# A decoder trunk step on one core: who sums the squares at the three phase boundaries, and with what the third unit opens

## The chip, the cores and the metric

One Trainium2 chip, one of its cores. The metric is the device time of one execution in microseconds (us), the median of the runs shown. Engines: TensorE (PE, with its weight loads as PEld), VectorE (DVE), ScalarE (ACT), GpSimd (POOL) and SyncE (SP), which issues most DMAs.

## The reference

One inference step of a two-layer trunk over 544 tokens (512 prompt tokens and 8 samples of 4), model width 1024, feed-forward width 2816. Cut to what matters:

```python
def rms_norm(x, g):
    y = x * rsqrt(mean(x * x, axis=-1) + EPS) * g

for l in range(2):
    h = rms_norm(x, norm_mix_pre[l])
    mix = mixer_ab(h, ...) if l == 0 else mixer_c(h, ...)     # in_ab/out_ab, in_c/out_c
    x = x + rms_norm(mix, norm_mix_post[l])
    h = rms_norm(x, norm_ffn_pre[l])
    a, b = split(h @ w_up)
    fo = (gelu(conv3(a)) * b) @ w_down                         # up0/down0, up1/down1
    x = x + rms_norm(fo, norm_ffn_post[l])
```

So in front of each of up0, in_c and up1 there are two norms in a row: the post-norm of the phase that ends, whose result is added to x, and the pre-norm of the new x, which feeds the next projection.

## The kernel before, in words

Activations lie feature by token: 8 row tiles (k = 0 to 7) of 128 partitions by 544 tokens. A bank of PSUM holds 272 columns of float32 here, so the tokens are cut in two halves, t = 0 and t = 1 (`cols(t)`). Every product is made of three passes of a split number, h_hi x w_hi, h_lo x w_hi and h_hi x w_lo, in `half` (L435 to L454). A *unit* is 128 output features over all k; its two halves e = 0, 1 are four k each, 24 products of 272 columns. Units use the accumulators `acc[0]` and `acc[1]` in turn (u % 2), each of two banks, one for each t. The semaphore `evac` counts accumulators that VectorE has emptied; before unit u PE waits until unit u-2 has been emptied (L681).

Eight phases follow each other: in_ab, out_ab, up0, down0, in_c, out_c, up1, down1. PE, VectorE, ScalarE and GpSimd each run their own program in order; what comes first on an engine is the order written out in its block, and all else is semaphores.

**The pre-norm is applied behind the projection.** h_hi and h_lo hold x times the gain, without the root; the results are multiplied by `rstd` when they leave PSUM. So products of the next phase start before the norm is known. The norm needs, for each half t, the sum of squares over all 1024 features: ScalarE writes the squares to `sq_c` (L1082, signal `sq_pre`); PE sums them in `square_sums` (L520 to L529), eight products with a 128 x 32 matrix of ones into four groups of 32 partitions, so that four partial sums stand there 32 times each; ScalarE copies this to `S[2]` (`sums_out`, L920, signal `sums_taken`); PE sums over partitions with a 128 x 128 matrix of ones (`pre_stats`, L531 to L534, signal `stat_done`); ScalarE makes the root with Ln and Exp (`norm_root`, L911 to L918, signal `rstd_ready`). Since every sum is then held 32 times, the scale in Ln is 1/(32 D).

**The first two units** of such a phase are interleaved with these steps (`first_pair`, L478 to L512): first all of t = 0 for both units, as its h tiles come, with the last post-norm statistics `stats(norm - 1, 1)` behind four of its products; then `square_sums` of t = 0; then t = 1, k by k for both units, with `pre_stats` of t = 0 behind k = 4, `square_sums` of t = 1 ahead of k = 7, and `pre_stats` of t = 1 at the end. VectorE copies each accumulator out whole (L1413), unscaled, and multiplies by `rstd` when the root is there (L1678 in up phases, L1836 in in_c). `third_unit` (L514) waits for the first of these copies, then makes the first half of the third unit.

**What follows in an up phase.** Units 2j and 2j+1 make the two sides of gate pair j. For each pair, in this order: VectorE empties the even unit times rstd into `S[0]` (L1700; for pair 0 it is the copy and L1678), GpSimd takes the columns of the samples (L1994 to L1998), ScalarE makes one tap of the convolution (L1170), VectorE the others (L1382 to L1386), ScalarE the gelu (L1174), GpSimd multiplies it with rstd (L2042), VectorE empties the odd unit times this (L1706; for pair 0 L1682), ScalarE rounds it to g_hi (L1180), VectorE subtracts (L1708, L1684). Between these stand the splits of the weights to come: ScalarE rounds (L876), VectorE subtracts (L1364), half a unit at a time. Unit 4 waits for L1700 of unit 2, unit 5 for L1706 of unit 3.

**In in_c** a head is four units; behind the units of the first head PE makes transposes (L808) of `kd`, at the end of a chain of scans and exponentials on VectorE and ScalarE that starts at L1836.

ScalarE's and VectorE's sides of the boundaries are `after_out` (behind out_ab and out_c) and `after_down` (behind down0).

Of the kernel before, what the change touches and what calls it, by code (L numbers as in the profile page):

```python
# [173 lines left out]
def build(nc, dram):  # L174
# [11 lines left out]
    with ctx:  # L186
# [119 lines left out]
        sq_summed, sums_taken = sem("sq_summed"), sem("sums_taken")  # L306
        stat_done = sem("stat_done")
# [126 lines left out]
        def _(pe):  # L434
# [43 lines left out]
            def first_pair(name, norm):  # L478

                m = 2 * UNIT0[name]  # L480
                if norm == 0:
                    for k, u in [(0, 0), (1, 0), (0, 1), (1, 1)] + [(k, u) for k in range(2, 8) for u in range(2)]:
                        e = k // 4
                        half(m + 2 * u + e, 0, u, h, 4 * e, e == 0, e == 1, tile_ready(0) if u == 0 else None,
                             ks=[k % 4], signal={(0, 3): 1, (0, 7): 1, (1, 7): 2}.get((u, k), 0))
                    for t in range(2):
                        stats(0, t)
                    return
                pre = norm // 2
                if pre == 2:  # L490
                    pe.wait_ge(evac, TILE0[name] - 1)
                for e in range(2):
                    for u in range(2):
                        if (e, u) == (0, 1):
                            pe.wait_ge(mix_cols, COLS0[pre + 1])
                        for k in range(4):
                            half(m + 2 * u + e, 0, u, h, 4 * e, e == 0, e == 1, half_ready(pre, 0) if u == 0 else None,
                                 ks=[k], signal=0, ts=(0,))
                        if (e, u) == (0, 0):
                            stats(norm - 1, 1)  # L500
                square_sums(pre, 0)
                pe.wait_ge(evac, TILE0[name])
                for k in range(8):
                    e = k // 4
                    if k == 7:
                        square_sums(pre, 1)
                    for u in range(2):
                        half(m + 2 * u + e, 0, u, h, 4 * e, e == 0, e == 1, half_ready(pre, 1) if u == 0 else None,
                             ks=[k % 4], signal={(0, 3): 1, (0, 7): 1, (1, 7): 2}.get((u, k), 0), ts=(1,))
                    if k == 4:  # L510
                        pre_stats(pre, 0)
                pre_stats(pre, 1)  # L512

            def third_unit(name):  # L514

                m = 2 * (UNIT0[name] + 2)
                pe.wait_ge(evac, TILE0[name] + 1)
                half(m, 0, 0, h, 0, True, False)

            def square_sums(pre, t):  # L520

                sq = sq_c
                pe.wait_ge(rstd_ready, 4 * pre - 2 + t + 1)
                for k in range(KD):
# [4 lines left out]
                mm.then_inc(sq_summed, 1)  # L529
# [145 lines left out]
            def ffn(layer):  # L675
# [10 lines left out]
                third_unit(name)  # L686
                half(2 * (UNIT0[name] + 2) + 1, 0, 0, h, 4, False, True)
# [169 lines left out]
        def _(act):  # L857
# [53 lines left out]
            def norm_root(norm, out, t):  # L911

                pre = norm % 2 == 0 and norm > 0
                src = A[2 + t if pre else t][:, 0:H]
                act.wait_ge(stat_done, 2 * norm + t + 1)
                step.mark(act.activation(out[:, cols(t)], src, ACT.Ln, bias=eps[:], scale=1.0 / (32 * D if pre else D)))
# [3 lines left out]
            def sums_out(pre, t):  # L920

                act.wait_ge(sq_summed, 2 * pre - 1 + t)
                act.copy(S[2][:, cols(t)], A[2 + t][:, 0:H]).then_inc(sums_taken, 1)

# [159 lines left out]
            def after_out(out, post, gain, name):  # L1084
# [19 lines left out]
                for k in range(KD):  # L1104
                    normed_tile(pre, 1, k, gain)
                    normed_square(1, k)
                    if k == 4:
                        sums_out(pre, 0)
                norm_root(2 * pre, rstd, 0)
                sums_out(pre, 1)  # L1110
                norm_root(2 * pre, rstd, 1)

            def after_down(post, gain=None, name=None):
# [20 lines left out]
                norm_root(post, S[3], 1)  # L1134
                for k in range(KD):
                    normed_tile(pre, 1, k, gain)
                    normed_square(1, k)
                    if k == 4:
# [213 lines left out]
        def _(dve):  # L1352
# [65 lines left out]


# [248 lines left out]
            def ffn(layer):  # L1668
                name = f"up{layer}"

                def first_unit(t):

                    pair = CA + KF * layer
                    if t == 1:
                        dve.wait_ge(sp_ready, pair)
                        first_pair(name, (S[0][:], S[3][:]))
                        dve.wait_ge(rstd_ready, 2 * (3 + 4 * layer))
                        dve.tensor_tensor(S[0][:], S[0][:], rstd[:], ALU.mult).then_inc(rescaled, 1)  # L1678
# [32 lines left out]
                base = step.n  # L1711
                up(0, 0, True)
                per = step.n - base
                base = step.n
# [114 lines left out]
            def head_out(t, cur):  # L1829
# [3 lines left out]
                if isinstance(cur, int) and cur == 0 and t == 1:  # L1833
                    first_pair("in_c", (S[0][:], qn[:]))
                    dve.wait_ge(rstd_ready, 10)
                    dve.tensor_tensor(S[0][:], S[0][:], rstd[:], ALU.mult).then_inc(rescaled, 1)  # L1836
# [338 lines left out]
```

## Time and profile before

| | us |
|---|---|
| median of 3 runs | 1331.42 (1331.3 to 1331.63) |
| profiled execution, own time | 1331.55 |
| its span in the profile | 1329.8 |
| PE busy | 1309.1 (98%) |
| DVE busy | 802.4 (60%) |
| ACT busy | 595.7 (45%) |
| POOL busy | 187.0 (14%) |

TensorE's granted clock is at its upper level, 2.4 GHz, throughout (0.998 in the mean). Products are pipelined: a row of 0.29 us stands for one product of 272 columns, but the next begins 0.125 us later, so for PE the distance between starts counts and not the duration. A row "x2" groups two products. A bracket "[0.66 <-ACT ...]" at the end of a row is the engine's idle time before it and what ended it.

### The profile page before, as it was taken

What the parts mean: (1) busy time and instruction counts of PE and PEld (TensorE: products, weight loads), DVE (VectorE), ACT (ScalarE), POOL (GpSimd) and SP (SyncE); (2) the same over time, 40 slices, a digit from 0 to 9 for tenths busy, and PEclk for the clock granted to TensorE, in tenths of its full rate; (3) what the DMA queues carried; (4) which work ended last, traced back from release to release, by engine and by line L of the source; (5) the groups of instructions that cost most, each with busy time, mean ns of one, the idle gap of its engine ahead of it and who ended that gap; (6) DMA issues with size and microseconds to landing.
All of it is one profiled execution on the core that took longest, in us unless ns stands there. A gap on an engine that the chain in (4) does not pass through costs nothing.

```text
span 1329.8 us, 31828 instructions
## 1 busy us (share of the span) xinstructions
PE 1309.1 (98%) x12588; PEld 1278.5 (96%) x12588; DVE 802.4 (60%) x1458; ACT 595.7 (45%) x1207; POOL 187.0 (14%) x320
## 2 busy tenths in 40 slices
PE   9999999999999999999999999999999999999997
PEld 9988999999999999997999999989999999999996
DVE  6476576655655632238988888968565565552224
ACT  5367355333333322237666666646433333332231
POOL 0111121111111100000211111111111111120000
PEclk9999999999999999999999999999999999999999
DMA  8311221323222322212333233331123322332212
GB/s 293 116 49 65 82 95 51 92 95 92 81 82 92 123 89 88 81 50 87 115 110 99 97 97 103 108 118 60 53 90 95 93 80 81 98 122 89 89 41 68
DMA packets 39685, 123.23 MB, mean 93 GB/s; under 512 B 4232, under 2 KB 12168, under 8 KB 39496
## 3 DMA queue, kind: packets, MB, share of 16 engines
q1 hardware_dynamic: 35400, 111.92, 26.7%
q10 hardware_dynamic: 4048, 10.00, 2.2%
q8 instruction: 44, 0.72, 0.2%
q0 software_dynamic: 176, 0.44, 0.1%
q14 instruction: 17, 0.14, 0.0%
HBM read 113.78 MB, written 8.57 MB: 92 GB/s over the span
## 4 chain that ended last, share of the span: by engine, by line
PE 91%; DVE 4%; ACT 2%; issue 1%; DMA 0%; POOL 0%; ACTq 0%; SPq 0%; DVEq 0%
PE acc L449 85%; PE aux L753 1%; DVE w_lo L1364 1%; PE aux L606 1%; PE aux L781 0%; PE aux L737 0%; DVE x L1586 0%; DMA raw<-in_w_in_ab 0%; DVE mix L1581 0%; PE aux L527 0%; PE aux L628 0%; PE aux L618 0%; DVE h_lo L1373 0%; ACT w_hi L876 0%; PE aux L545 0%
## 5 line engine op out<-in xcount | busy, mean ns | idle before, releaser
L1364 DVE TENSOR_TENSOR w_lo<-raw,w_hi 128x512 fp32r<-128x512 f32 (+1 forms) x372 | 305.4, 825 | 321.9 <-ACT w_hi L876 321.8
L449 PE MATMUL acc<-h_hi,w_hi 128*128 128x272 f32 x2208 | 474.5, 293 | 3.3 <-DVE h_lo L1373 2.5
L449 PE MATMUL acc<-h_hi,w_lo 128*128 128x272 f32 x2208 | 464.7, 288 | 0.0
L449 PE MATMUL acc<-h_lo,w_hi 128*128 128x272 f32 x2208 | 463.3, 288 | 0.5 <-issue 0.5
L449 PEld LDWEIGHTS acc<-h_hi,w_hi 128*128 128x128 f32 x2208 | 349.6, 188 | 15.4 <-issue 7.5
L876 ACT CAST w_hi<-raw 128x512 fp32r<-128x512 f32 (+1 forms) x372 | 236.3, 642 | 264.1 <-PE acc L449 258.4
L449 PEld LDWEIGHTS acc<-h_lo,w_hi 128*128 128x128 f32 x2208 | 349.9, 189 | 0.2
L449 PEld LDWEIGHTS acc<-h_hi,w_lo 128*128 128x128 f32 x2208 | 348.0, 189 | 0.6 <-issue 0.6
L449 PE MATMUL acc<-g_hi,w_hi 128*128 128x272 f32 x704 | 153.0, 288 | 0.0
L449 PE MATMUL acc<-g_hi,w_lo 128*128 128x272 f32 x704 | 153.0, 289 | 0.0
L449 PE MATMUL acc<-g_lo,w_hi 128*128 128x272 f32 x704 | 152.4, 288 | 0.0
L449 PEld LDWEIGHTS acc<-g_hi,w_hi 128*128 128x128 f32 x704 | 113.4, 188 | 0.1
L449 PEld LDWEIGHTS acc<-g_lo,w_hi 128*128 128x128 f32 x704 | 113.4, 189 | 0.1
L449 PEld LDWEIGHTS acc<-g_hi,w_lo 128*128 128x128 f32 x704 | 112.7, 189 | 0.0
L2042 POOL TENSOR_TENSOR scratch<-scratch,rstd 128x544 f32<-128x544 f32 x44 | 60.0, 1364 | 169.1 <-ACT scratch L1174 169.1
L1174 ACT ACTIVATE scratch<-scratch 128x544 f32<-128x544 f32 x44 | 29.0, 659 | 112.3 <-DVE scratch L1386 112.3
L1180 ACT CAST g_hi<-scratch 128x544 f32 (+1 forms) x44 | 28.5, 647 | 98.2 <-DVE scratch L1706 93.7
L449 PE MATMUL acc<-y_hi,w_hi 128*128 128x272 f32 x256 | 69.9, 292 | 1.7 <-DVE y_lo L1889 1.3
L449 PE MATMUL acc<-y_hi,w_lo 128*128 128x272 f32 x256 | 68.9, 288 | 0.0
L449 PE MATMUL acc<-y_lo,w_hi 128*128 128x272 f32 x256 | 68.8, 288 | 0.0
L1170 ACT ACTIVATE scratch<-scratch,vec 128x544 f32<-128x544 f32 x44 | 33.0, 751 | 65.7 <-DVE scratch L1700 64.0
L1987 POOL TENSOR_TENSOR scratch<-scratch 128x272 f32<-128x272 f32 (+1 forms) x30 | 31.2, 1038 | 198.6 <-ACT scratch L1036 151.2
(255 smaller groups left out, 1339.6 us busy)
## 6 DMA issues: line engine op xcount, KB each, us to landing
raw<-in_w_up SPq DMA_DIRECT2D x88, 512.0 KB, 3.6
raw<-in_w_down SPq DMA_DIRECT2D x32, 704.0 KB, 4.1
raw<-in_w_in_c SPq DMA_DIRECT2D x32, 512.0 KB, 3.7
raw<-in_w_in_ab SPq DMA_DIRECT2D x18, 512.0 KB, 3.8
raw<-in_w_out_ab SPq DMA_DIRECT2D x8, 512.0 KB, 3.6
S<-in_state ACTq DMA_DIRECT2D x8, 512.0 KB, 3.6
o_ss<-Snew ACTq DMA_DIRECT2D x8, 512.0 KB, 2.7
raw<-in_w_out_c SPq DMA_DIRECT2D x8, 512.0 KB, 3.5
```

What stands on the lines that cost most here:

```text
L449: mm = pe.matmul(acc[out][:, t, 0:H], w[slot][:, wc], mv[:, kk_, t * H:(t + 1) * H], start=start and k == 0 and q == 0, stop=stop and k == ...
L606: mm = pe.matmul(A[g][:, j * 256 + lo_k:j * 256 + 256], q_sb[rows, 2 * pair + j, n * WIN:(n + 1) * WIN], k_sb[rows, (n - 1) * WIN + lo_k:( ...
L753: mm = pe.matmul(A[2 * (c % 2)][half_, to], kt[of_chunk(c), n, half_], vt[of_chunk(c), n, :], start=True, stop=True)
L876: act.copy(w_hi[slot][:, to:to + kts * P], raw[n % 4][:, cols]).then_inc(hi_ready, 1)
L1170: act.activation(S[1][:], S[0][:], ACT.Copy, scale=vec[:, bass.ds(w + u + 2 * i, 1)]).then_inc(tap_ready, 1)
L1174: act.activation(S[2][:], S[1][:], ACT.Gelu_apprx_tanh).then_inc(act_done, 1)
L1180: act.copy(g_hi[:, u + 2 * i, :], S[3][:]).then_inc(g_hi_ready, 1)
L1364: dve.tensor_tensor(w_lo[slot][:, to], raw[n % 4][:, cols], w_hi[slot][:, to], ALU.subtract).then_inc(lo_ready, 1)
L1987: pool.tensor_tensor(S[2][:, q], S[2][:, q], S[k % 2][:, q], ALU.add).then_inc(sq_added, 1)
L2042: pool.tensor_tensor(S[2][:], S[2][:], rstd[:], ALU.mult).then_inc(gate_ready, 1)
```

## The change

1. **Up phases, second half (t = 1):** PE's `square_sums(pre, 1)` goes. VectorE adds the eight squares itself in three additions (`squares_added`: 4 x 272, 2 x 272, 272 columns) and writes `S[2]`; ScalarE's `sums_out(pre, 1)` goes there, and the scale in Ln is 1/D for that half. `pre_stats(pre, 1)` moves from the end of `first_pair` to behind `third_unit`.
2. **in_c, second half:** `square_sums` is issued in two groups, tiles 0 to 3 ahead of k = 5 and tiles 4 to 7 ahead of k = 7. ScalarE's `sums_out(pre, 1)` stands ahead of the root of the first half and no longer behind it.
3. **All three boundaries:** the bank of unit 0 for t = 0 is copied out early by ScalarE (`first_cols`, at k = 2 of the second half); VectorE copies only the t = 1 columns of that unit. `third_unit` starts with k = 0, 1 of t = 0, which waits for ScalarE's copy alone, then waits for VectorE's copy and does k = 0, 1 of t = 1, then k = 2, 3 of both.
4. **All three:** the last post-norm statistics stand behind three products of the first unit and no longer behind four. In `after_down` ScalarE's root of these statistics moves from behind the first half's tiles to behind tile 6.

```diff
@@ first_pair (PE)
-                                 ks=[k], signal=0, ts=(0,))
-                        if (e, u) == (0, 0):
-                            stats(norm - 1, 1)
-                square_sums(pre, 0)
+                                 ks=[k], signal=0, ts=(0,), done=first_cols_done if (e, u, k) == (1, 0, 3) else None)
+                            if (e, u, k) == (0, 0, 2):
+                                stats(norm - 1, 1)
+                square_sums(pre, 0, range(KD))
...
-                    if k == 7:
-                        square_sums(pre, 1)
+                    if name == "in_c" and k == 5:
+                        square_sums(pre, 1, range(4))
+                    if name == "in_c" and k == 7:
+                        square_sums(pre, 1, range(4, KD))
...
-                pre_stats(pre, 1)
+                if name == "in_c":
+                    pre_stats(pre, 1)
@@ third_unit (PE)
+                pe.wait_ge(first_cols_copied, RESCALED[name] // 2)
+                for k in range(2):
+                    half(m, 0, 0, h, 0, True, False, ks=[k], signal=0, ts=(0,))
                 pe.wait_ge(evac, TILE0[name] + 1)
-                half(m, 0, 0, h, 0, True, False)
+                for k in range(2):
+                    half(m, 0, 0, h, 0, True, False, ks=[k], signal=0, ts=(1,))
+                half(m, 0, 0, h, 0, True, False, ks=range(2, 4))
@@ ffn (PE)
                 third_unit(name)
+                pre_stats(norm // 2, 1)
                 half(2 * (UNIT0[name] + 2) + 1, 0, 0, h, 4, False, True)
@@ ScalarE
+            def first_cols(pre):
+                act.wait_ge(first_cols_done, pre)
+                act.copy(S[0][:, cols(0)], acc[0][:, 0, 0:H]).then_inc(first_cols_copied, 1)
@@ after_out (ScalarE)
+                    if k == 2:
+                        first_cols(pre)
...
                 norm_root(2 * pre, rstd, 0)
-                sums_out(pre, 1)
                 norm_root(2 * pre, rstd, 1)
@@ after_down (ScalarE)
-                norm_root(post, S[3], 1)
+                    if k == 6:
+                        norm_root(post, S[3], 1)
...
+                    if k == 2:
+                        first_cols(pre)
...
+                sums_out(pre, 1)
                 norm_root(2 * pre, rstd, 0)
-                sums_out(pre, 1)
                 norm_root(2 * pre, rstd, 1)
@@ first_pair (VectorE)
                     dve.wait_ge(half_done, m + 2 * u + 2)
+                    if u == 0 and name != "in_ab":
+                        dve.tensor_copy(out[:, cols(1)], acc[0][:, 1, 0:H]).then_inc(evac, 1)
+                        if name != "in_c":
+                            squares_added(RESCALED[name] // 2)
+                        continue
                     dve.tensor_copy(tok2(out), acc_v[u]).then_inc(evac, 1)
+            def squares_added(pre):
+                q = cols(1)
+                dve.wait_ge(sq_pre, x_count(pre, 1, KD - 1))
+                step.mark(dve.tensor_tensor(sq_c[:, 0:4, q], sq_c[:, 0:4, q], sq_c[:, 4:8, q], ALU.add))
+                step.wait(dve)
+                step.mark(dve.tensor_tensor(sq_c[:, 0:2, q], sq_c[:, 0:2, q], sq_c[:, 2:4, q], ALU.add))
+                step.wait(dve)
+                dve.wait_ge(sums_taken, {1: 1, 3: 5}[pre])
+                dve.tensor_tensor(S[2][:, q], sq_c[:, 0, q], sq_c[:, 1, q], ALU.add).then_inc(sums_taken, 1)
```

The rest of the diff is waits that keep the order: VectorE's rescales also wait for `first_cols_copied`, and the counts of the semaphores follow.

## Rows read from the trace of the kernel before

**Rows 1.** The page's busy table: busy us, share of the span, instructions.

```profile
PE 1309.1 (98%) x12588; PEld 1278.5 (96%) x12588; DVE 802.4 (60%) x1458; ACT 595.7 (45%) x1207; POOL 187.0 (14%) x320
```

**Rows 2.** Waits of PE, whole kernel: us in total, times, longest us.

```profile
PE acc L449 <- DVE h_lo L1373: 2.5, 6, 1.5
```

**Rows 3.** Timeline of PE at up0's first pair: start us, us, engine, line, operands.

```profile
208.92 0.29 PE L449 MATMUL acc<-h_hi,w_lo 128*128 128x272 f32 x1
...
209.63 0.29 PE L449 MATMUL acc<-h_lo,w_hi 128*128 128x272 f32 x1
...
210.88 0.29 PE L449 MATMUL acc<-h_hi,w_lo 128*128 128x272 f32 x1
211.10 1.12 PE L527 MATMUL aux<-sq_c,ones 128*32 128x272 f32 x16
...
212.15 0.39 PE L449 MATMUL acc<-h_hi,w_hi 128*128 128x272 f32 x1
212.38 0.29 PE L449 MATMUL acc<-h_lo,w_hi 128*128 128x272 f32 x1
...
213.00 0.62 PE L534 MATMUL aux<-scratch,ones 128*128 128x272 f32 x2
```

**Rows 4.** Timelines of ACT, DVE and POOL around and behind it; the last row is up1's.

```profile
208.49 0.52 ACT L1077 ACTIVATE h_hi<-x,vec 128x272 fp32r<-128x272 f32 x1 [0.33 <-DVE x L1586]
...
212.90 1.36 DVE L1413 COPY scratch<-acc 128x544 f32<-128x544 f32 x2 [2.16 <-PE acc L449]
214.71 0.72 DVE L1678 TENSOR_TENSOR scratch<-scratch,rstd 128x544 f32<-128x544 f32 x1 [0.46 <-ACT rstd L918]
...
223.68 0.72 DVE L1700 TENSOR_TENSOR scratch<-acc,rstd 128x544 f32<-128x544 f32 x1
...
228.96 1.37 POOL L2042 TENSOR_TENSOR scratch<-scratch,rstd 128x544 f32<-128x544 f32 x1 [3.47 <-ACT scratch L1174]
...
229.42 1.46 DVE L1364 TENSOR_TENSOR w_lo<-raw,w_hi 128x512 fp32r<-128x512 f32 x1 [1.23 <-ACT w_hi L876]
230.80 0.71 DVE L1706 TENSOR_TENSOR scratch<-acc,scratch 128x544 f32<-128x544 f32 x1
...
242.72 0.71 DVE L1706 TENSOR_TENSOR scratch<-acc,scratch 128x544 f32<-128x544 f32 x1
...
950.08 0.71 DVE L1706 TENSOR_TENSOR scratch<-acc,scratch 128x544 f32<-128x544 f32 x1
```

**Rows 5.** Timeline of PE: the first products of units 4 and 5 of up0.

```profile
225.81 0.41 PE L449 MATMUL acc<-h_hi,w_hi 128*128 128x272 f32 x2
...
231.82 0.41 PE L449 MATMUL acc<-h_hi,w_hi 128*128 128x272 f32 x2
```

**Rows 6.** Groups of VectorE's instructions by form: count, busy us, mean ns, idle before.

```profile
L1581 DVE TENSOR_TENSOR mix<-mix,scratch 128x272 f32<-128x272 f32 x48 | 20.8, 434 | 7.1 <-ACT scratch L918 7.1
...
L1866 DVE TENSOR_TENSOR vbd<-v_s,own 96x1024 fp32r<-96x1024 f32 x8 | 10.0, 1250 | 0.0
```

**Rows 7.** Timeline of PE at in_c: k = 4 of t = 1, statistics, third unit, transposes.

```profile
615.00 0.36 PE L449 MATMUL acc<-h_hi,w_hi 128*128 128x272 f32 x1 [0.24 <-DVE h_lo L1373]
...
619.79 0.62 PE L534 MATMUL aux<-scratch,ones 128*128 128x272 f32 x2
620.44 0.49 PE L449 MATMUL acc<-h_hi,w_hi 128*128 128x272 f32 x2
...
630.36 0.66 PE L808 MATMUL aux<-ident,c_kd 128*128 128x128 f32 x4 [0.66 <-ACT c_kd L1296]
```

**Rows 8.** Timelines of ACT and DVE at in_c's first half and its last root.

```profile
605.79 0.52 ACT L1077 ACTIVATE h_hi<-x,vec 128x272 fp32r<-128x272 f32 x1 [0.94 <-DVE x L1586]
...
606.54 0.47 ACT L916 ACTIVATE scratch<-aux,eps 128x272 f32<-128x272 f32 x1
...
607.50 0.44 DVE L1581 TENSOR_TENSOR mix<-mix,scratch 128x272 f32<-128x272 f32 x1 [0.65 <-ACT scratch L918]
...
620.44 0.49 ACT L916 ACTIVATE rstd<-aux,eps 128x272 f32<-128x272 f32 x1 [0.98 <-PE aux L534]
```

More of the change, by code:

```diff
@@ L306, in build @@
         sq_summed, sums_taken = sem("sq_summed"), sem("sums_taken")
+        first_cols_done, first_cols_copied = sem("first_cols_done"), sem("first_cols_copied")
         stat_done = sem("stat_done")
@@ L511, in first_pair, with square_sums @@
                         pre_stats(pre, 0)
-                pre_stats(pre, 1)
+                if name == "in_c":
+                    pre_stats(pre, 1)
             def third_unit(name):
                 m = 2 * (UNIT0[name] + 2)
+                pe.wait_ge(first_cols_copied, RESCALED[name] // 2)
+                for k in range(2):
+                    half(m, 0, 0, h, 0, True, False, ks=[k], signal=0, ts=(0,))
                 pe.wait_ge(evac, TILE0[name] + 1)
-                half(m, 0, 0, h, 0, True, False)
-            def square_sums(pre, t):
+                for k in range(2):
+                    half(m, 0, 0, h, 0, True, False, ks=[k], signal=0, ts=(1,))
+                half(m, 0, 0, h, 0, True, False, ks=range(2, 4))
+            def square_sums(pre, t, ks):
                 sq = sq_c
-                pe.wait_ge(rstd_ready, 4 * pre - 2 + t + 1)
-                for k in range(KD):
+                if 0 in ks:
+                    pe.wait_ge(rstd_ready, 4 * pre - 2 + t + 1)
+                for k in ks:
                     j = k % 4
@@ L528, in square_sums @@
                                    start=k < 4, stop=k >= 4)
-                mm.then_inc(sq_summed, 1)
+                if KD - 1 in ks:
+                    mm.then_inc(sq_summed, 1)
             def pre_stats(pre, t):
@@ L914, in norm_root @@
                 src = A[2 + t if pre else t][:, 0:H]
+                by_tiles = pre and (t == 0 or norm == 4)
                 act.wait_ge(stat_done, 2 * norm + t + 1)
-                step.mark(act.activation(out[:, cols(t)], src, ACT.Ln, bias=eps[:], scale=1.0 / (32 * D if pre else D)))
+                step.mark(act.activation(out[:, cols(t)], src, ACT.Ln, bias=eps[:],
+                                         scale=1.0 / (32 * D if by_tiles else D)))
                 step.wait(act)
@@ L920, in sums_out @@
             def sums_out(pre, t):
-                act.wait_ge(sq_summed, 2 * pre - 1 + t)
+                act.wait_ge(sq_summed, {1: 1, 2: 2, 3: 4}[pre] + t)
                 act.copy(S[2][:, cols(t)], A[2 + t][:, 0:H]).then_inc(sums_taken, 1)
+            def first_cols(pre):
+                act.wait_ge(first_cols_done, pre)
+                act.copy(S[0][:, cols(0)], acc[0][:, 0, 0:H]).then_inc(first_cols_copied, 1)
             act.dma_start(x[:, 0, :], dram["xT"][:, 0, :]).then_inc(x_in[0], 16)
@@ L1677, in first_unit @@
                         dve.wait_ge(rstd_ready, 2 * (3 + 4 * layer))
+                        dve.wait_ge(first_cols_copied, RESCALED[name] // 2)
                         dve.tensor_tensor(S[0][:], S[0][:], rstd[:], ALU.mult).then_inc(rescaled, 1)
@@ L1709, in up @@
                                                   ).then_inc(g_ready, 1)
-                base = step.n
                 up(0, 0, True)
-                per = step.n - base
-                base = step.n
+                base, per = step.n, 4
                 with dve.Fori(1, KF // 2 - 1) as i:
@@ L1835, in head_out @@
                     dve.wait_ge(rstd_ready, 10)
+                    dve.wait_ge(first_cols_copied, 2)
                     dve.tensor_tensor(S[0][:], S[0][:], rstd[:], ALU.mult).then_inc(rescaled, 1)
```

## The prediction

> **What bounds the kernel now.** I read the page's busy table first: TensorE (PE) is busy for 98% of the span [rows 1], so only what shortens or stalls PE's own stream can count. The table of PE's waits over the whole kernel comes next. Its longest entry is 2.5 us, for `h_lo` tiles [rows 2]; nearly all of that belongs to the boundary in front of `in_c`. Between the two up phases' first products and their ends PE waits for nothing. But a stream without waits says nothing about how narrowly it misses them, so for each `evac` wait of PE I read two timelines side by side: when PE arrives, and when VectorE (DVE) has the accumulator free. Three boundaries are touched: up0 (near 211 us), in_c (near 615 us), up1 (near 930 us). up1 repeats up0's rows 719.28 us later (`L1706` at 230.80 and at 950.08 [rows 4]), so I cost up0 and take it twice.
>
> **Up phases, what PE saves.** In the stream, the eight squares products take 212.38 - 210.88 = 1.50 us from the last product before to the second one behind, where two products take 0.25: 1.25 us [rows 3]. They go, so k=7 starts at 210.88 + 0.125 = 211.01 and its six products end at 211.76. A statistics product (`pre_stats`) costs by the same sum 209.63 - 208.92 - 0.25 = 0.46 us; it stays, but later. The third unit no longer waits for a 544-column copy: before, from the statistics at 213.00 to unit 4 at 225.81 [rows 5] PE took 12.81 us, for 96 products (12.03, at the 0.1253 us that units 4 and 5 keep) and 0.46 of statistics; the other 0.32 us were that wait. Its first six products use the half of the bank that ScalarE (ACT) has long copied and run 211.76 to 212.51. The DVE copy of the other half begins 0.39 us behind the start of u=0's last product (before: product at 212.51, the one after 212.38, and copy at 212.90 [rows 3, 4]), so at 211.26 + 0.39 = 211.65, plus 0.44 (the 272-column form [rows 6]) is 212.09. No wait. Unit 2's first half is 24 products of 0.1253 us, 3.01 us, so it ends at 214.77; statistics 0.46, then 72 products, 9.02 us: PE arrives at unit 4 at **224.25**, where it arrived at 225.81 [rows 5]. That is 1.56 us earlier.
>
> **Up phases, what moves.** The second statistics product now stands behind these 24 products: it was issued at 213.00 and will be at **214.77, 1.77 us later**. DVE's three adds (1088, 544, 272 columns) must be done by then. From 0.72 us for 544 (`L1678` [rows 4]) and 0.434 for 272 [rows 6], a column costs 1.05 ns: 1088 take about 1.29 us, and the 1024-column form, 1.25 us, agrees [rows 6]. 212.05 + 1.29 + 0.72 + 0.44 + three hand-overs of 0.04 is 214.6 us: 0.15 us in time. Queued behind the adds on DVE are the copy of u=1 (done by 215.35; PE wants that bank only at 218.2) and the rescale, which waits for the root anyway. ACT's extra copy (0.4 us at most) lies in the idle 0.33 us that ACT has before a tile of h_hi [rows 4], and can make one tile late by 0.1 us; PE takes that tile 0.7 us after it is ready or later.
>
> Who waits for the statistics? ACT's root, the rescale `L1678` at 214.71, GpSimd's sample columns, the convolution, gelu, the gate product, `g_lo`, two weight splits, and only then `L1700` at 223.68, which frees the bank of unit 4, and, after another such round, `L1706` at 230.80, which frees the bank of unit 5 [rows 4]. I looked for a link that hangs on anything but its predecessor and found none: each begins within 0.1 us of the last one's end, or behind DVE's own splits, which are in the same chain. So the whole chain moves by 1.77 us.
> - Unit 4: bank free at 223.68 + 0.72 + 1.77 = 226.17; PE arrives at 224.25, waits, starts at 226.2 (before 225.81).
> - Unit 5: bank free at 230.80 + 0.71 + 1.77 = 233.28; PE would arrive at 226.2 + 6.02 = 232.2, and starts at 233.32, plus 0.10 us for refilling (behind a break in the stream the first two products stand 212.38 - 212.15 = 0.23 us apart [rows 3], else 0.125): 233.42, where it was 231.82 [rows 5]. **PE is 1.60 us later than before.**
> - Unit 7: bank free at 242.72 + 0.71 + 1.77 = 245.20, PE arrives at 233.42 + 12.03 = 245.45. No further wait, and a round of the chain (242.72 - 230.80 = 11.92 us) is shorter than one of PE (12.03), so the room grows from there.
>
> Even with no delay at all the saving had nowhere to go: before, unit 5's bank came at 231.51 and PE at 231.82, 0.3 us of room for 1.56 us of haste. The two up phases cost 2 x 1.60 = **+3.2 us**; by the ends of what I don't know (adds late or not, refill 0 or 0.1) +2.9 to +3.6.
>
> The sample of `w_lo` at 229.42 that takes 1.46 us where 512 columns cost 0.69 by the price above, beside GpSimd's 1.37 us at 228.96 [rows 4], belongs to the chain; both hang on the same gelu and move together, so it is neither saved nor added.
>
> **in_c.** The post-norm statistics move ahead of k=3, into PE's longest wait (1.5 us [rows 2]), and ACT's root moves to k=6, into the 0.94 us that ACT idles before 605.79 [rows 8]. The root took 606.54 to 607.50; now DVE can begin the second half right behind the last `h_lo`. Its idle 0.65 us before 607.50 go [rows 8], and 0.09 us by which instructions that wait for nothing overlap: 0.74 us earlier. PE's product k=4 (615.00) then begins at 614.26; from there PE is bound by itself. The squares in two groups do the same work, with one more change of shape: about +0.10 us. So the last statistics product goes from 619.79 to 619.15, 0.64 us earlier. ACT now does sums, first root, second root in a row: sums done near 618.8, first root 0.93, second at about 619.8, when its statistics are there: a tie. The third unit starts 0.25 us behind the statistics, at 619.4 instead of 620.44 [rows 7], 1.04 us earlier, but the transposes at 630.36 wait 0.66 us for `kd` [rows 7], whose chain begins at the root; it gains only 0.64. Their wait grows to about 1.06, and the boundary is worth **-0.64 us** (from 0, if the three ACT steps in a row run late, to -1.04, PE's whole gain).
>
> **Sum.** +3.2 - 0.64 = +2.56 us. Profiled execution: 1331.55 (span 1329.8), to 1334.1. On the median of 1331.42: **1334.0 us**, +0.19%.
>
> **Rivals.**
> - *A: PE's saving is kept.* PE is the busiest engine by far, and the change takes products off it: 2 x 1.56 + 1.04 = 4.2 us, 1327.3 us. It decides at unit 4 and 5: the chain would have to free their banks by 224.2 and 230.3, 0.2 and 1.2 us before it does now [rows 4, 5], though its root is asked for later. Chance 0.05. The Trainium skill ("Perfetto Trace Analysis", Identifying the Most-Contended Engine) says to optimize the engine with the highest occupancy first; by that rule this rival is the expected outcome, and the rows of the chain speak against it here.
> - *B: the chain has room that I don't see,* so the up phases come out even (a link held back by something of PE's that now comes early). 1331.42 - 0.64 = 1330.8 us; partly, up to 1332. Against it: the idle times before each link name the link before. Chance 0.12.
> - *C: DVE's adds are late.* Room is 0.15 us. Slowed like the `w_lo` of rows 4, by 0.77 us, they push the statistics, the chain and PE by 0.6 us more in each phase: 1335.2 us. Against it: GpSimd has nothing to do then. Chance 0.08.
> - *D: as forecast, but in_c gains nothing:* the second root is late because ACT does the first one behind the sums. 1334.6 us. Chance 0.13.
>
> **How the numbers follow.** Forecast 0.62, its own range 1333.3 to 1334.6. The range for 8 in 10 takes in D, most of C and the upper part of B: 1331.9 to 1335.2, and leaves out A and the rest of B. About 0.2% (2.66 us) is what a measurement of this kernel can tell from no change; that line, 1334.08, runs through my forecast. Faster 0.06 (A and a little), slower 0.42 (the upper third of the forecast, 0.22, C and nearly all of D), within it 0.52.
>
> **What the profile would show.** Right: a wait of PE of about 2 us for `L1700` and one of about 1 us for `L1706` in each up phase, none before; `L1678` 1.8 us later than 214.71; the third unit's first product near 211.8. At in_c: `L1581` of the second half without its 0.65 us idle, and the transposes' wait for `kd` near 1 us. Wrong: no PE wait at units 4 and 5 (A or B); the second statistics product behind a wait for DVE (C); in_c's second root at or behind 620.44 (D).

## The result, and the profile after

The kernel after takes **1334.51 us** in the median of 7 runs (1334.01 to 1337.52), the kernel before, run beside it, 1331.30 (1330.8 to 1332.05). The medians are 0.24% apart; the ratio on record, taken over all these runs, is 1.0028 with a 95% interval of 1.0018 to 1.0038: a small loss, but clear of no change. The forecast was 1334.0 with a range of 1331.9 to 1335.2. The profiled execution of after took 1334.01 us with a span of 1332.2; that of before 1331.55 and 1329.8.

TensorE (PE) does less work and the time is longer. The page's busy table of after (busy us, share of the span, instructions), against [rows 1]:

```profile
PE 1307.3 (98%) x12556; PEld 1277.6 (96%) x12556; DVE 806.0 (61%) x1464; ACT 595.3 (45%) x1208; POOL 186.5 (14%) x320
```

32 PE instructions less are the eight squares products, of two instructions each, in two up phases. Where the time went stands at the top of the table of PE's waits (us in total, times, longest):

```profile
PE acc L450 <- DVE scratch L1740: 3.7, 2, 1.9
PE acc L450 <- DVE scratch L1746: 1.7, 2, 0.8
...
PE acc L450 <- DVE y_lo L1928: 0.8, 1, 0.8
PE aux L820 <- ACT c_kd L1319: 0.7, 1, 0.7
```

The first two lines are new; in [rows 2] the largest entry is 2.5 us for `h_lo`. L1740 and L1746 are L1700 and L1706 of before, the emptyings that unit 4 and unit 5 of an up phase wait for. Each stands there twice, once for each up phase. Below are the timelines of up0, first DVE's, then PE's (its last row is up1's); the third fence is one PE row of before that [rows 5] doesn't show. A row gives start, duration, engine and line, and the bracket is the idle time before and what ended it.

```profile
211.66 0.44 DVE L1437 COPY scratch<-acc 128x272 f32<-128x272 f32 x1 [1.31 <-PE acc L450]
212.02 1.28 DVE L1452 TENSOR_TENSOR sq_c<-sq_c 128x1088 f32<-128x1088 f32 x1
...
214.09 0.44 DVE L1457 TENSOR_TENSOR scratch<-sq_c 128x272 f32<-128x272 f32 x1
...
216.48 0.73 DVE L1718 TENSOR_TENSOR scratch<-scratch,rstd 128x544 f32<-128x544 f32 x1 [1.31 <-issue]
...
225.43 0.72 DVE L1740 TENSOR_TENSOR scratch<-acc,rstd 128x544 f32<-128x544 f32 x1
...
232.54 0.71 DVE L1746 TENSOR_TENSOR scratch<-acc,scratch 128x544 f32<-128x544 f32 x1
```

```profile
211.76 0.29 PE L450 MATMUL acc<-h_hi,w_hi 128*128 128x272 f32 x1
...
214.78 0.62 PE L545 MATMUL aux<-scratch,ones 128*128 128x272 f32 x2
...
224.01 0.41 PE L450 MATMUL acc<-h_hi,w_lo 128*128 128x272 f32 x2
226.28 0.51 PE L450 MATMUL acc<-h_hi,w_hi 128*128 128x272 f32 x2 [1.86 <-DVE scratch L1740]
...
233.38 0.51 PE L450 MATMUL acc<-h_hi,w_hi 128*128 128x272 f32 x2 [0.83 <-DVE scratch L1746]
233.73 0.41 PE L450 MATMUL acc<-h_lo,w_hi 128*128 128x272 f32 x2
...
953.45 0.51 PE L450 MATMUL acc<-h_hi,w_hi 128*128 128x272 f32 x2 [0.83 <-DVE scratch L1746]
```

```profile
232.07 0.41 PE L449 MATMUL acc<-h_lo,w_hi 128*128 128x272 f32 x2
```

The third unit opens at 211.76 without a wait, and the adds end at 214.53. The statistics product is issued at 214.78, where it was 213.00 [rows 3]. From there each step is later by nearly the same amount: the rescale 216.48 against 214.71, L1740 225.43 against 223.68, L1746 232.54 against 230.80 [rows 4], that is +1.77, +1.75, +1.74. PE could have started unit 4 at 224.01 + 0.25 = 224.26 and starts at 226.28. (The bracket's 1.86 us count from the end of the row before, 224.42; in a stream the next pair would have begun before that end.) Unit 5 starts at 233.38 against 231.82 [rows 5], **1.56 us later**. Behind each stop the first pair takes 0.35 us where the stream takes 0.25, so the row behind it, 233.73 against 232.07, is 1.66 us later. That is what an up phase costs: 1.67 us from there to the next boundary, as the row at the end of down0 shows below. up1 repeats it with the same two waits.

At in_c the rows that answer to [rows 7, 8] follow, behind the row by which the arrival is compared, VectorE's first copy of this boundary at the end of down0; its row in the kernel before comes first:

```profile
590.65 0.44 DVE L1560 COPY mix<-acc 128x272 f32<-128x272 f32 x1 [6.77 <-PE acc L449]
```

```profile
592.32 0.44 DVE L1599 COPY mix<-acc 128x272 f32<-128x272 f32 x1 [6.78 <-PE acc L450]
...
603.67 0.73 PE L556 MATMUL aux<-scratch,ones 128*128 128x272 f32 x2 [0.58 <-ACT scratch L1068]
...
608.43 0.44 DVE L1620 TENSOR_TENSOR mix<-mix,scratch 128x272 f32<-128x272 f32 x1
...
615.91 0.36 PE L450 MATMUL acc<-h_hi,w_hi 128*128 128x272 f32 x1 [0.24 <-DVE h_lo L1396]
...
621.04 0.62 PE L545 MATMUL aux<-scratch,ones 128*128 128x272 f32 x2
...
621.36 0.42 PE L450 MATMUL acc<-h_hi,w_hi 128*128 128x272 f32 x1
...
621.70 0.49 ACT L929 ACTIVATE rstd<-aux,eps 128x272 f32<-128x272 f32 x1
...
622.74 0.73 DVE L1875 TENSOR_TENSOR scratch<-scratch,rstd 128x544 f32<-128x544 f32 x1 [0.77 <-ACT rstd L932]
...
623.86 1.29 DVE L1387 TENSOR_TENSOR w_lo<-raw,w_hi 128x512 fp32r<-128x512 f32 x2
...
624.60 0.52 PE L450 MATMUL acc<-h_hi,w_hi 128*128 128x272 f32 x2
...
631.60 0.66 PE L820 MATMUL aux<-ident,c_kd 128*128 128x128 f32 x4 [0.72 <-ACT c_kd L1319]
```

The work arrives there 1.67 us late, from up0 (592.32 against 590.65). Less that, the second half's first addition (608.43) is 0.74 us earlier than before, k=4 (615.91) 0.76, but the statistics product (621.04) only 0.42, and the transposes (631.60) 0.43. So the rows give +1.67 - 0.43 + 1.67 = +2.91 us.

The profiled executions differ by 2.46 us. The other 0.45 are one wait outside the change: that for `y_lo` behind the heads is 1.26 us in the profile of before and 0.8 to 0.9 in those of all ten other kernels; two of these, the doses below, have before's code there. (The first weights' split, too, holds PE for 0.3 us in one profile and for 2.1 in another, but all that is over long before up0.)

The medians differ by 3.2 us. A part of that is TensorE's clock. Of after's seven executions the two with a mean granted clock of 0.998 took 1334.01 and 1334.22 us, the two with 0.995 took 1335.0 and 1335.18, and one with 0.994 took 1337.52, while every execution of before on record with its clock has 0.997 or 0.998. A trace further below, of a kernel close to after, shows what such a fall is and what it costs.

Since arrivals differ between executions, stretches are compared below by their distance from a common row: in up0 DVE's first copy (211.66 in after, 212.90 in before) or, where a kernel moves that, the statistics product of the first half (209.05 in both); at in_c the statistics product L556 or the copy at the end of down0. "On after's clock" means shifted by that distance.

### The profile page after: what moved, and what is told of

The parts are those of the page before. It is cut to its first block, busy times and chain, and to the rows that moved or that the text cites. A ratio compares the mean times of both kernels' runs of the same rounds, so it can differ in the third digit from the quotient of the medians.

```text
span 1332.2 us, 31774 instructions
## 1 busy us (share of the span) xinstructions
PE 1307.3 (98%) x12556; PEld 1277.6 (96%) x12556; DVE 806.0 (61%) x1464; ACT 595.3 (45%) x1208; POOL 186.5 (14%) x320
## 4 chain that ended last, share of the span: by engine, by line
PE 87%; DVE 7%; ACT 3%; issue 2%; POOL 1%; DMA 0%; SPq 0%; DVEq 0%; ACTq 0%; POOLq 0%
PE acc L450 81%; DVE w_lo L1387 1%; ACT w_hi L888 1%; PE aux L617 1%; PE aux L765 0%; DVE x L1625 0%; DMA raw<-in_w_in_ab 0%; PE aux L749 0%; PE aux L793 0%; DVE mix L1620 0%; PE aux L639 0%; DVE h_lo L1396 0%; PE aux L629 0%; DVE Sst L1799 0%; PE aux L556 0%
```

## The experiments

The theory is that of the prediction: the chain from the second statistics product through L1718 and L1740 to L1746 sets the start of unit 5, PE's saved products matter for nothing there, and the chain starts 1.77 us late because PE issues that product behind 24 others. The place and the adds can't be parted in the kernel after, though: DVE's sums are there at 214.53, so the product could have been issued at most 0.25 us earlier wherever it stood. Its rivals: PE's stream itself (products saved or split in halves) has become slower; DVE's adds are late or hold up what is queued behind them.

### The up phases' squares on PE again

```diff
-                    if name == "in_c" and k == 7:
-                        square_sums(pre, 1, range(4, KD))
+                    if k == 7:
+                        square_sums(pre, 1, range(4, KD) if name == "in_c" else range(KD))
...
-                if name == "in_c":
-                    pre_stats(pre, 1)
+                pre_stats(pre, 1)
...
-                pre_stats(norm // 2, 1)
...
-                        if name != "in_c":
-                            squares_added(RESCALED[name] // 2)
```

The part not shown brings back ScalarE's copy of the sums and the scale in Ln.

> The changed kernel with one part undone: in the up phases PE sums the squares of the second half again, with its statistics product in front of the third unit, as before; the new opening of the third unit, the early root and in_c's two groups stay. Theory (the chain behind the second statistics product decides): statistics of up0 near 213.0 us again, so the bank of unit 5 is free near 231.5 as before; PE reaches it up to 0.3 us earlier and gains at most 0.2 us in each up phase; with in_c's 0.3 the time is 0.3 to 0.8 us below before, 1330.5 to 1331.0. Rival (the loss comes from the third unit's split opening or from ScalarE's extra copy): the waits at units 4 and 5 stay and the time stays near 1334. Rival (PE's own products decide): 1.05 us of products come back in each phase, so the time is 2 us above the changed kernel, 1336.5.

Measured: 1330.8 us (11 runs, 1330.3 to 1330.96) beside 1331.38 of before, ratio 0.9995 (0.9986 to 1.0004).

```profile
213.07 0.62 PE L544 MATMUL aux<-scratch,ones 128*128 128x272 f32 x2
...
223.74 0.72 DVE L1737 TENSOR_TENSOR scratch<-acc,rstd 128x544 f32<-128x544 f32 x1
...
230.85 0.71 DVE L1743 TENSOR_TENSOR scratch<-acc,scratch 128x544 f32<-128x544 f32 x1
...
231.69 0.51 PE L450 MATMUL acc<-h_hi,w_hi 128*128 128x272 f32 x2
```

The divided copy and the opening with first-half products are still in this kernel, and it is not slower. They are cleared: the loss comes with the statistics product's new place or with the adds. The last row shows how narrow it was in the kernel before. This execution arrives 0.07 us late; less that, unit 5 starts 0.20 us ahead of [rows 5], because the third unit no longer waits for the whole copy, and then it has met the chain: it starts 0.13 us behind L1743's end at 231.56, the same distance as in after (L1746 ends at 233.25, unit 5 starts at 233.38). Before had the bank at 231.51, so with this hand-over its room was 231.82 - 231.51 - 0.13 = 0.18 us, not 0.3. With the slower first pair a net 0.10 us is left in each up phase; with in_c's 0.43 that makes 0.63, where the medians differ by 0.58, which the interval alone could not tell from nothing.

### The statistics product late, with no adds: two doses

The kernel before, its squares on PE as they were, with the up phases' second statistics product behind 6 or behind all 24 products of the third unit's first half. The edit for 24; for 6 the product stands inside `third_unit`, behind its first k:

```diff
-                pre_stats(pre, 1)
+                if name == "in_c":
+                    pre_stats(pre, 1)
...
                 third_unit(name)
+                pre_stats(norm // 2, 1)
```

> The kernel before with one edit: in the up phases the second statistics product stands behind the first 6 products of the third unit; nothing is added or taken away. Theory: it is issued near 214.42 instead of 213.00, 1.42 us later; unit 5's bank comes at 231.51 + 1.42 = 232.93 and unit 5 starts near 233.05, 1.2 us later than before, in each of two phases: 2.4 us in all, 1333.7. Rival (PE's own products or VectorE's adds decide): nothing changes, 1331.3.

> The kernel before with one edit: in the up phases the second statistics product stands behind all 24 products of the third unit's first half. Theory: issued near 216.7 instead of 213.00, 3.7 us later; unit 5 starts near 235.3, 3.5 us later than before, 7.0 us in the two phases: 1338.3; with the run that delays by 1.4 us, one us of delay costs one us once the room of 0.3 us is used. Rival (PE's own products or VectorE's adds decide): nothing changes, 1331.3.

Measured: 1334.08 us (10 runs), ratio 1.002 (1.0011 to 1.0029), and 1338.87 (4 runs), ratio 1.0058 (1.0043 to 1.0073). PE and DVE with the dose of 24 (this execution is 0.30 us late on arrival, first copy at 213.20; that with the dose of 6 is 0.08 early, 212.82):

```profile
217.09 0.62 PE L535 MATMUL aux<-scratch,ones 128*128 128x272 f32 x2
...
218.80 0.73 DVE L1680 TENSOR_TENSOR scratch<-scratch,rstd 128x544 f32<-128x544 f32 x1 [4.24 <-ACT rstd L920]
...
228.62 0.51 PE L449 MATMUL acc<-h_hi,w_hi 128*128 128x272 f32 x2 [1.88 <-DVE scratch L1702]
...
235.72 0.51 PE L449 MATMUL acc<-h_hi,w_hi 128*128 128x272 f32 x2 [0.83 <-DVE scratch L1708]
```

With 24 products PE's two waits are 1.88 and 0.83 us, those of after to 0.02, and unit 5 starts 235.72 - 0.30 - 231.82 = 3.60 us later than in [rows 5], for a statistics product that is 3.79 us later. With 6 products unit 4 finds its bank free, and unit 5 waits 0.71 us and starts at 233.06, 1.32 us later for 1.53: in both the delay less 0.2 us of room. Neither kernel has an add on DVE. So a statistics product that comes late is enough; the adds aren't needed for it. With the 0.10 us of the first pair, two phases make 2.84 and 7.40 us, and the medians say 2.70 and 7.49. The distance from statistics to unit 5 is 235.72 - 217.09 = 18.63 us with 24 products, 233.06 - 214.45 = 18.61 with 6, and 233.38 - 214.78 = 18.60 in the kernel after: one chain of fixed length.

### The root early on ScalarE undone; one group of squares

Two looks at in_c, each with one edit of after undone:

```diff
-                    if k == 6:
-                        norm_root(post, S[3], 1)
+                norm_root(post, S[3], 1)
```

```diff
-                    if name == "in_c" and k == 5:
-                        square_sums(pre, 1, range(4))
                     if name == "in_c" and k == 7:
-                        square_sums(pre, 1, range(4, KD))
+                        square_sums(pre, 1, range(KD))
```

> The kernel after with ScalarE's second root of the feed-forward's output back behind the last tile (one edit of the change undone, in front of the heads). If that root is what brings VectorE's second half forward, the first addition of the second half comes at about 609.1 instead of 608.43, the second statistics product at about 621.7 instead of 621.04, and the time about 0.6 over the kernel after. If it brings nothing, nothing moves.

> The kernel after with the squares of the second half summed in one group of eight ahead of the head's phase, as before the change. If the split into two groups costs the 0.3 us by which the second statistics product there gained less than VectorE's work did, that product comes at about 620.7 instead of 621.04, and the first wait for kd ends 0.3 us earlier; time about 0.3 under the kernel after. If the groups are free, both stay where they are.

Measured with the late root, 1334.82 us in one run; this execution arrives 0.38 us ahead of after's (L556 at 603.29 against 603.67):

```profile
608.79 0.44 DVE L1619 TENSOR_TENSOR mix<-mix,scratch 128x272 f32<-128x272 f32 x1 [0.66 <-ACT scratch L932]
...
621.40 0.62 PE L545 MATMUL aux<-scratch,ones 128*128 128x272 f32 x2
...
631.96 0.66 PE L820 MATMUL aux<-ident,c_kd 128*128 128x128 f32 x4 [0.72 <-ACT c_kd L1318]
```

DVE's idle 0.66 us is back, and on after's clock the three rows are at 609.17, 621.78 and 632.34: the early root is worth 0.74 us at each. With one group, 1334.96 us in one run; it arrives 0.81 us late (L554, which is L556 in after, at 604.48):

```profile
619.60 1.12 PE L535 MATMUL aux<-sq_c,ones 128*32 128x272 f32 x16
...
621.51 0.62 PE L543 MATMUL aux<-scratch,ones 128*128 128x272 f32 x2
...
632.07 0.66 PE L818 MATMUL aux<-ident,c_kd 128*128 128x128 f32 x4 [0.72 <-ACT c_kd L1317]
```

On after's clock 620.70 and 631.26: both 0.34 us earlier. The squares in two groups cost 0.34 us, and 0.74 - 0.34 = 0.40 is the boundary's gain, where the direct comparison with before gives 0.42 to 0.43. The single times settle nothing here, as they differ by less than the spread of after's own runs; the rows do.

The 0.81 us of this execution hold something else. It enters up0 0.36 us late (first copy at 212.02); the other 0.45 come from PE's stream behind the stop at unit 4. The rows are PE's timeline, the last line is a view by stretches: from, to, length, then busy us of PE, PEld, DVE, ACT and POOL, and then the granted clock, 0.50:

```profile
226.65 0.51 PE L450 MATMUL acc<-h_hi,w_hi 128*128 128x272 f32 x2 [1.87 <-DVE scratch L1738]
...
228.63 0.66 PE L450 MATMUL acc<-h_hi,w_lo 128*128 128x272 f32 x2
```

```profile
228.00:230.00 2.00, 2.00 (x11) 2.00 (x11) 1.97 (x4) 0.00 (x0) 0.00 (x0) 0.50 0.50 201
```

From about 227.3 to 230.45 us the granted clock is 0.50, the lower level of 1.2 GHz, and pairs start 0.45 us apart instead of 0.25. It falls again at the same place in up1 (0.50 from 948 to 950 us), and once in the run with the late root, in up1 only. Both stand behind a stop of PE of 1.86 to 1.87 us; after's profile has two such stops and no fall, so the stop doesn't bring it each time. All kernels with the long stop (after, the dose of 24 and these two) have executions with a mean clock of 0.994 to 0.998; the 61 executions of the other six kernels on record, whose stops at units 4 and 5 are at most 0.95 us in their profiles, all have 0.997 or 0.998. The two falls in up1 cost 0.45 and 0.43 us (from the first half's statistics product of up1 to VectorE's last row 399.82 and 399.80 us, in after 399.37). Two of them make 0.9, and 0.9 is what after's executions at 0.995 lie above those at 0.998. So the change has a second price, outside the sum, that a profile without a fall doesn't show.

### Taking steps out of the chain

If the chain sets unit 5, shortening it must give PE's saving back. First the weight splits of units 4 and 5, moved ahead on ScalarE and VectorE into the time in which both wait for the root, with a wait on the products that read those buffers last:

```diff
                 norm_root(2 * pre, rstd, 0)
+                for q in range(8, 12):
+                    split(m + q, 0, m + 4)
                 norm_root(2 * pre, rstd, 1)
...
                         first_pair(name, (S[0][:], S[3][:]))
+                        for q in range(8, 10):
+                            split(2 * UNIT0[name] + q, 0)
...
```

VectorE's splits 10 and 11 and the lines that skip the old places are cut here.

> The changed kernel, and the weight splits of units 4 and 5 are taken out of the chain in up phases: ScalarE rounds all four halves ahead of the last root, where it idles 4.5 us; VectorE subtracts two ahead of the rescale, one behind the first convolution, one while ScalarE rounds g. Theory: the chain to unit 4 is shorter by about 1.2 us, that to unit 5 by about 2.5. Unit 4 waits until about 225.0, unit 5 starts without a wait near 231.1, 0.7 us earlier than before; two phases and in_c's 0.3 give 1.7 us below before: 1329.6. Rival (the chain has other links that hold it): a wait stays at unit 5, and the time is 1331 or more. Rival (the loss of the changed kernel is PE's refill or VectorE's load): as the changed kernel, 1334, or worse, since VectorE has less idle time.

Measured: 1329.85 us (11 runs, 1328.96 to 1331.3), ratio 0.9988 (0.9979 to 0.9997). Unit 5 starts without a wait at 231.49 on after's clock, expected 231.1. The chain to unit 4 became 0.91 us shorter, not 1.2:

```profile
215.84 1.29 DVE L1393 TENSOR_TENSOR w_lo<-raw,w_hi 128x512 fp32r<-128x512 f32 x2
...
219.05 0.75 DVE L1411 SCALAR_TENSOR_TENSOR scratch<-scratch,vec 128x511 f32<-128x511 f32 x1 [1.27 <-ACT scratch L1199]
...
226.01 0.51 PE L450 MATMUL acc<-h_hi,w_hi 128*128 128x272 f32 x2 [0.95 <-DVE scratch L1751]
```

The convolution starts 219.05 - 217.06 = 1.99 us behind the rescale, in the kernel after 218.12 - 216.48 = 1.64: of the 1.20 us of splits taken out, 0.35 are lost there. ScalarE's tap, which it waits for, ends 1.50 us behind the rescale in both; what holds the convolution for the rest is open. The direction was right, the size too big.

Then what frees unit 2's accumulator, L1740 itself. In the order written out it stands behind `g_lo` of pair 0, yet it needs only unit 2 and an `S[0]` that the convolution has read. It goes directly behind the convolution, into the 2.16 us in which DVE waits for GpSimd's gate product; alone, and with the early splits:

```diff
                             if t == 2:
                                 conv(S[0], col(w, j), col(w + KF, j), pair, pair)
+                                if first and u == 0:
+                                    dve.wait_ge(conv_done, pair + 1)
+                                    dve.wait_ge(half_done, 2 * UNIT0[name] + 6)
+                                    dve.tensor_tensor(tok2(S[0][:]), acc_v[0], tok2(rstd[:]), ALU.mult).then_inc(evac, 1)
...
-                            if t == 1:
+                            if t == 1 and not (first and u == 1):
```

> The kernel after with only the emptying of unit 2 moved behind the first pair's convolution; the splits stay where they are. Chain theory: PE's wait for L1740 goes, and what is late next is VectorE's split of the fifth unit's weights (it starts at 224.2 and takes 0.64 us a half), so unit 4 starts at about 225.0; ScalarE's tap of the second pair comes 1.5 us earlier, the emptying for unit 5 at about 231.0, unit 5 at about 231.8, as in the kernel before; time 1331.3. If instead both halves of the split must be done, unit 4 starts at 225.6 and unit 5 at 231.9 to 232.3, time 1331.5 to 1332.3. If the second emptying does not come earlier, unit 5 stays at 233.4 and the time at 1334.5.

> The kernel after with the splits of units 4 and 5 out of the chain, and VectorE's emptying of unit 2 moved from behind g_lo to right behind the first pair's convolution, into the time in which VectorE waits for GpSimd's gate (2.16 us idle in the kernel after). The chain theory (what is late after this change is the emptying that unit 4 and then unit 5 wait for): PE starts unit 4 without a wait, unit 5 at about 230.7 (before 231.8, after 233.4, early splits 231.5), and the time is about 1328.2, 0.8 us per up phase under the run with the early splits alone. A rival, that TensorE's work or the weights' transfers would bound the phases by then: unit 5 stays at 231.5 or gets a new wait, and the time stays at 1329.8.

Measured alone: 1330.88 us (11 runs), ratio 0.9999 (0.999 to 1.0008).

```profile
219.60 0.72 DVE L1746 TENSOR_TENSOR scratch<-acc,rstd 128x544 f32<-128x544 f32 x1
...
224.54 0.52 PE L450 MATMUL acc<-h_hi,w_hi 128*128 128x272 f32 x2 [0.55 <-DVE w_lo L1387]
...
231.28 0.51 PE L450 MATMUL acc<-h_hi,w_hi 128*128 128x272 f32 x2 [0.46 <-DVE scratch L1750]
```

L1746 is the moved emptying here, L1750 that of unit 3. This execution is 0.43 us early, so unit 4 starts at 224.97 behind the split of its first weights (expected 225.0) and unit 5 at 231.71 (expected 231.8): 1.67 us earlier than in after, by moving one instruction.

Measured with the early splits: **1327.58 us** (10 runs, 1327.09 to 1329.2) beside 1331.2 of before, ratio 0.9974 (0.9965 to 0.9984). PE's table of waits has no entry for either emptying (L1757 and L1761 here), and its timeline runs through:

```profile
214.79 0.62 PE L545 MATMUL aux<-scratch,ones 128*128 128x272 f32 x2
...
220.31 0.72 DVE L1757 TENSOR_TENSOR scratch<-acc,rstd 128x544 f32<-128x544 f32 x1
...
224.27 0.41 PE L450 MATMUL acc<-h_hi,w_hi 128*128 128x272 f32 x2
...
229.08 0.72 DVE L1761 TENSOR_TENSOR scratch<-acc,scratch 128x544 f32<-128x544 f32 x1 [2.24 <-POOL scratch L2096]
...
230.28 0.41 PE L450 MATMUL acc<-h_hi,w_hi 128*128 128x272 f32 x2
```

With the statistics at 214.79, as late as in after (214.78), unit 4 starts at 224.27 and unit 5 at 230.28, 1.54 us ahead of [rows 5] in each up phase. PE's busy us from 224 to 236 is 12.00 where after has 9.32. I had expected unit 5 at 230.7 and 1328.2 us; it gained the whole 3.1 us against after's 233.38. DVE's adds are in this kernel as in after, so what is queued behind them doesn't cost the time either.

### Everything, with one group of squares

> The kernel after with the early splits, the early emptying and the squares ahead of the heads in one group of eight. Chain theory: the gains add up, as they lie in different phases; the up phases as in the kernel with the early emptying (no wait of TensorE at units 4 and 5), the second statistics product ahead of the heads and the first wait for kd 0.34 us earlier; time about 1327.2. If the one group's gain is lost in the heads (a later wait takes it up), the time stays at 1327.6.

Measured: 1327.45 us (8 runs, 1327.05 to 1328.81) beside 1331.31 of before, ratio 0.9973 (0.9962 to 0.9983). From the statistics product L556 or L554 of the boundary to the second one it takes 17.04 us (617.42 - 600.38), in the kernel without this edit 17.37 (617.83 - 600.46), and the wait for `kd` ends 27.59 us behind it against 27.93: the 0.34 us is there in the rows. In the time, 0.13 us between two medians of separate sets of runs on two chips, it can't be told.

## Why the prediction was right, point by point

- **What PE saves.** Forecast: third unit at 211.76, statistics at 214.77, PE at unit 4 at 224.25. Measured 211.76, 214.78 and 224.26 (224.27 in the kernel that doesn't stop). The 1.25 us for eight products, read from the distances of starts, held.
- **The chain.** Forecast +1.77 us on each link, measured 1.77, 1.75 and 1.74. Unit 5 forecast at 233.42, measured 233.38. The doses without adds confirm it, and the kernels that shorten the chain give the saving back. Shown. Two small terms were misplaced and nearly cancel at unit 5: the hand-over from the emptying to PE is 0.13 us and not 0.04, and the slow first pair comes behind unit 5's start and not ahead of it. The cost of an up phase is 1.67 us, forecast 1.60.
- **The adds.** Forecast 1.29 us for 1088 columns and done by 214.6; measured 1.28 and 214.53. The room of 0.25 us was a little wider than the 0.15 reckoned. Rival C falls.
- **Unit 7.** No wait, as forecast: the next rounds of the chain run without PE waiting for either emptying.
- **in_c.** The sign was right, the size too big: -0.64 forecast, -0.43 measured. The step that failed is the term "The squares in two groups ... about +0.10 us". They cost 0.34, as two pairs of kernels show; the gain in front of them was 0.74 to 0.76, as forecast (0.74). One part of the 0.34 can be seen: at each change from products to squares and at each change back, one start comes 0.22 us behind the last where the stream has 0.125 (619.38 to 619.60, 620.19 to 620.42), and the second group adds one change of each kind, 0.2 us in all. What the rest is wasn't measured.
- **The wait for `kd`**, forecast to grow to about 1.06 us, grew to 0.72. PE's own stream gained less there than the 1.04 us reckoned: 0.42 up to the statistics, and hardly more behind them. Its last product ahead of the transposes starts at 630.47; less 1.67, that is 0.49 us before the 629.29 of the kernel before, and 0.66 + 0.49 - 0.43 = 0.72. The opening of the third unit does come 0.33 us sooner behind the statistics, but its second half, at 624.60, begins with two starts 0.34 and 0.35 us apart instead of 0.25. No wait is listed there. By the order in the program PE needs VectorE's split of this half's weights just then: the first of the two at 623.86, at 0.69 us each, ends at 624.55, 0.05 us ahead of PE's start, the same distance as where a wait for such a split is listed (0.04 at 224.54, in the kernel with only the emptying moved). That split stands behind the rescale L1875, so it comes no earlier than the root allows. No run moves it, so this is read and not tested. ScalarE's three steps in a row were the tie that was forecast (sums 620.33, roots 620.61 and 621.70): the second root begins 0.66 us behind its statistics product, before 0.65, and rival D falls.
- **The sum.** +3.2 - 0.64 = +2.56 was forecast; the rows give +3.34 - 0.43 = +2.91, less 0.45 us of `y_lo`'s wait, which differs between the two executions, 2.46, as in the profiles. The median of 1334.51 lies another half us above the profiled execution: that half is not in the forecast's terms, and the falls of the clock behind PE's stop, put at nothing, account for part of it.
- **Rival A** gave 1327.3 us if the chain freed its banks by 224.2 and 230.3. By the Trainium skill ("Perfetto Trace Analysis", Identifying the Most-Contended Engine) the engine with the highest occupancy comes first, TensorE judged by MFU and the busy share of its weight loads (96% here). The change followed that and lost; the kernel whose chain meets those two times runs at 1327.58. So the trace agrees with that rule only once the chain's 0.2 us of room had been widened: here it says where a gain can lie, not that it arrives.

## What to carry to other kernels

An engine that is 98% busy and waits for nothing can still have no room. Before taking work off it, read for each buffer it will ask for when that comes free: here 0.3 us of room, 0.2 with the hand-over, faced 1.56 us of haste. What the busy engine issues for others (a statistics product, 0.46 us of its time) belongs as early as its inputs allow, and each product put in front of it is paid at the end of the chain. In the kernel after that place was already nearly reached: work that moves from the fast engine to a slower one moves the chain's start with it, here from 213.00 to 214.53 at best. And where a chain has become the bound, look in the order written by hand for the instruction that frees the buffer and move it up into another wait: that one move was worth 3.6 us over the kernel after alone (3.3 by the rows), and with the splits it turned a ratio of 1.0028 into 0.9974.

## What the runs showed of the hardware

- A chain of more than a dozen instructions on four engines had the same length to 0.03 us in three kernels (18.60, 18.61 and 18.63 us).
- From the end of an emptying on VectorE to the first product of the unit that waits for it took 0.13 us, in two kernels (233.25 to 233.38 and 231.56 to 231.69), and the first pair behind the stop took 0.35 us instead of 0.25.
- TensorE's granted clock fell from 1.00 to 0.50 for about 3 us in some executions, behind a stop of 1.86 to 1.87 us; the stream ran at 0.45 us a pair instead of 0.25, and one fall cost 0.43 to 0.45 us. The profiles with stops of at most 0.95 us there have none in this stretch. Where the kernel before ends, the clock falls too: PE's last product starts at 1319.55, and from 1326 us on the granted clock is 0.50, so the word "throughout" above holds for it only up to there.
- Additions in float32 on VectorE cost the same per column up to 1088 columns: 0.44, 0.72 and 1.28 us for 272, 544 and 1088, that is 1.03 ns for a column and 0.16 us for each instruction.
- Breaking eight squares products into two runs of four, with ordinary products between, cost PE 0.34 us, more than the 0.10 that I had taken from the price of one change of shape.
